# Last attention values moved between branch b's products, branch c run one product further ahead, and the norm's gain applied by ScalarE while it rounds

## The reference

```python
def second_block(x, mem, positions, ...):
    x = x + 0.5 * swiglu(rmsnorm(x, ffn1_norm[l]), ffn1_w_gu[l], ffn1_w_down[l])
    h = rmsnorm(x, mix_norm[l])
    z = h @ w_in[l]
    ...
    y_a = spatial_gating(u, v, ...)            # branch a
    y_b = mla(...)                             # branch b, 8 heads
    y_c = memory_attention(...)                # branch c, 4 heads
    merged = (gates[:, :, 0] * (y_a @ w_branch_a[l])
              + gates[:, :, 1] * (y_b @ w_branch_b[l])
              + gates[:, :, 2] * (y_c @ w_branch_c[l]))
    x = x + merged @ w_out[l]
    x = x + 0.5 * swiglu(rmsnorm(x, ffn2_norm[l]), ffn2_w_gu[l], ffn2_w_down[l])

def rmsnorm(x, g):
    y = x * rsqrt(mean(x * x, axis=-1) + EPS)
    return y * g
```

## Time and profile before

| what | value |
|---|---|
| time, median of 3 runs (lowest to highest) | 1173.15 us (1172.92 to 1176.21) |
| the profiled execution: time, span of the profile | 1176.21 us, 1174.5 us |
| PE busy | 1106.4 us, 94% of the span |
| DVE, ACT, POOL busy | 694.7, 591.0, 440.2 us (59%, 50%, 37%) |
| mean granted clock of TensorE | 0.971 of full speed |
| DMA | 204.91 MB, mean 174 GB/s |

### The profile page before, as it was taken

One profiled execution on the slowest core, in us unless ns is written; L12 is line 12 of the kernel. 1 busy time (PEld: TensorE's weight loads), 2 busy tenths in 40 slices (PEclk: granted clock), 3 DMA queues, 4 the chain that ended last, 5 costly groups with the idle time before them and its releaser, 6 DMA issues.

```text
span 1174.5 us, 21772 instructions
## 1 busy us (share of the span) xinstructions
PE 1106.4 (94%) x8468; PEld 1065.5 (91%) x8468; DVE 694.7 (59%) x1122; ACT 591.0 (50%) x1041; POOL 440.2 (37%) x236
## 2 busy tenths in 40 slices
PE   4789999899989999999999999999999887999999
PEld 3669999778889999999999998999899887999998
DVE  6545878887668843337777423665766774444421
ACT  4436565564455554444444445697544345444432
POOL 5440112112544544434444453323323244444442
PEclk8889999899989999999999999999899998999999
DMA  9546977213435555555555554444233343555553
GB/s 366 211 144 222 355 264 271 92 56 125 162 128 183 189 183 179 182 178 180 181 185 185 186 179 137 168 137 169 99 120 132 120 153 126 188 179 180 183 186 117
DMA packets 57651, 204.91 MB, mean 174 GB/s; under 512 B 6959, under 2 KB 8367, under 8 KB 57432
## 3 DMA queue, kind: packets, MB, share of 16 engines
q1 hardware_dynamic: 51176, 180.53, 45.0%
q0 software_dynamic: 6384, 23.09, 5.5%
HBM read 202.53 MB, written 1.06 MB: 173 GB/s over the span
## 4 chain that ended last, share of the span: by engine, by line
PE 79%; DVE 9%; DMA 4%; ACT 3%; issue 2%; POOL 1%; SPq 1%; DVEq 0%; ACTq 0%; POOLq 0%
PE bank L613 79%; DMA ring<-in_stream 2%; DMA ada_ring<-in_ada 2%; DVE ring_rounded L1610 1%; DVE ada_acc L1687 1%; PE bank L867 1%; ACT rounded_rounded L1215 1%; POOL ring_rounded L1140 1%; ACT wide L1397 1%; DVE wide L1858 1%; DVE shared L2125 1%; DVE wide_rounded L1887 0%; DVE shared_rounded L1887 0%; SPq L567 0%; DVE stats L1853 0%
## 5 line engine op out<-in xcount | busy, mean ns | idle before, releaser
L1140 POOL TENSOR_TENSOR ring_rounded<-ring,rounded_rounded 128x1024 fp32r<-128x1024 f32 x154 | 386.5, 2510 | 595.5 <-ACT rounded_rounded L1215 595.5
L613 PE MATMUL bank<-u_rounded,rounded_rounded 128*128 128x256 f32 x1528 | 442.9, 290 | 6.1 <-ACT u_rounded L1272 3.8
L613 PE MATMUL bank<-u_rounded,ring_rounded 128*128 128x256 f32 x1528 | 436.3, 286 | 0.0
L613 PE MATMUL bank<-u_lo_rounded,rounded_rounded 128*128 128x256 f32 x1528 | 430.8, 285 | 0.0
L1215 ACT ACTIVATE rounded_rounded<-ring 128x1024 fp32r<-128x1024 f32 x326 | 340.9, 1053 | 166.8 <-PE bank L613 146.5
L1610 DVE TENSOR_TENSOR ring_rounded<-ring,rounded_rounded 128x1024 fp32r<-128x1024 f32 x172 | 255.5, 1487 | 213.2 <-ACT rounded_rounded L1215 212.8
L613 PEld LDWEIGHTS bank<-u_rounded,rounded_rounded 128*128 128x128 f32 x1528 | 297.8, 195 | 10.9 <-issue 9.7
L613 PEld LDWEIGHTS bank<-u_rounded,ring_rounded 128*128 128x128 f32 x1528 | 297.7, 195 | 0.1
L613 PEld LDWEIGHTS bank<-u_lo_rounded,rounded_rounded 128*128 128x128 f32 x1528 | 294.1, 194 | 1.4 <-DVE u_lo_rounded L1656 0.4
L613 PE MATMUL bank<-shared_rounded,rounded_rounded 128*128 128x256 f32 x992 | 256.6, 286 | 2.8 <-DVE wide L1900 2.6
L613 PE MATMUL bank<-wide_rounded,rounded_rounded 128*128 128x256 f32 x864 | 234.7, 287 | 18.3 <-DVE shared_rounded L1887 5.7
(11 more groups left out here) (273 smaller groups left out, 1149.5 us busy)
## 6 DMA issues: line engine op xcount, KB each, us to landing
ring<-in_stream SPq DMA_DIRECT2D x328, 512.0 KB, 3.3
ada_ring<-in_ada POOLq DMA_DIRECT2D x33, 512.0 KB, 5.6
wide<-in_mem_t SPq DMA_DIRECT2D x2, 512.0 KB, 5.9
shared<-in_ada POOLq DMA_DIRECT2D x2, 512.0 KB, 10.0
ada_ring<-in_ada SPq DMA_DIRECT2D x2, 512.0 KB, 13.7
x<-in_x_t SPq DMA_DIRECT2D x1, 1024.0 KB, 14.1
wide<-in_ada POOLq DMA_DIRECT2D x2, 512.0 KB, 21.4
wide<-in_ada SPq DMA_DIRECT2D x2, 512.0 KB, 21.5
```

The source lines that it names most:

```text
L613: return nc.tensor.matmul(out, lhs, rhs, start=start, stop=stop, skip_group_check=True)
L1140: pool.tensor_tensor(R(w), w, R(slot_round(q)), ALU.subtract).then_inc(slot_split_by_pool, 1)
```

## The change

Five edits:

1. PE: head i = 11's `values(10)`, `turn(11)` and `values(11)` no longer stand behind branch b's eight products but in front of `br_b3`, `br_b5` and `br_b7`; DVE's `split_output` of `memo2` and `memo3` moves in front of the gates of `br_b4` and `br_b7`.
2. PE and the weight stream: branch c's products stand in groups of 3, 2, 2, 1 (`C_BEFORE`) and not of 2, 2, 2, 2 before the steps of w_out.
3. The slot work of branch c's and `mix2_`'s tiles stands behind a tile's own work on DVE and ACT, not in front.
4. `add_and_split`: ACT rounds x times gain to u straight from x, with the gain as its per-partition scale, and only then squares; DVE's multiplication by the gain is gone, and its low part is one `scalar_tensor_tensor` (x times gain minus u).
5. The counters of `u_normed` are shifted for the row after ROW_2, which no longer counts there.

```diff
+C_BEFORE = ((0, 1, 2), (3, 4), (5, 6), (7,))
...
                     for m in range(KD):
+                        if m == 3:
+                            values(10)
+                        if m == 5:
+                            turn(11)
+                        if m == 7:
+                            values(11)
                         project(f"br_b{m}", 4, (attn_b, attn_b_lo2), ...)
                 if i < 11:
                     scores(i + 1)
-                if i:
-                    values(i - 1)
-                turn(i)
+                    if i:
+                        values(i - 1)
+                    turn(i)
...
-            values(11)
             for m in (0, 2, 4, 5):
                 claim(f"mix2_{m}")
             for k in range(KD // 2):
-                for m in (2 * k, 2 * k + 1):
+                for m in C_BEFORE[k]:
                     project(f"br_c{m}", 4, (attn_c, attn_c_lo2), ...)
...
             def round_merged(before, lo):
                 for m in range(KD):
-                    ahead(f"{'up_sb' if before == 0 else 'br_c'}{m}")
+                    if before == 0 or m == 0:
+                        ahead(f"{'up_sb' if before == 0 else 'br_c'}{m}")
                     act.wait_ge(merged_raw, before + m + 1)
                     a(R(merged[:, m, :]), lo[:, m, :], ACT.Copy).then_inc(merged_rounded, 1)
+                    if before and m < KD - 1:
+                        ahead(f"br_c{m + 1}")
...
-            def square_and_round(row, last, i):
-
-                taken(f"{last}{i}")
+            def round_and_square(row, last, i, gain, after):
+
+                if after is None:
+                    ahead(f"{last}{i}")
+                evacuated(act, f"{last}{i}")
+                a(R(u[:, i, :]), x[:, i, :], ACT.Copy, scale=col(gain, i)).then_inc(u_rounded, 1)
+                if after:
+                    ahead(after)
                 a(row_squares[:, i, :], x[:, i, :], ACT.Square).then_inc(row_squares_ready, 1)
-                act.wait_ge(u_normed, row * KD + i + 1)
-                a(R(u[:, i, :]), u_lo[:, i, :], ACT.Copy).then_inc(u_rounded, 1)
...
-                square_and_round(ROW_4, "mix2_", i)
+                round_and_square(ROW_4, "mix2_", i, "ffn2_norm_2", f"mix2_{min(i + 1, KD - 1)}")
...
-            def add_and_split(last, gate, gain, row):
+            def add_and_split(last, gate, gain, row, reach_later=False):
+
+                def low_part(i):
+                    dve.wait_ge(u_rounded, row * KD + i + 1)
+                    v.scalar_tensor_tensor(out=R(u_lo[:, i, :]), in0=x[:, i, :], scalar=gain[:, i:i + 1], in1=R(u[:, i, :]),
+                                           op0=ALU.mult, op1=ALU.subtract).then_inc(u_ready, 1)
...
                 for m in range(KD):
-                    add_residual(f"{last}{m}", m, gate(m), int(last == "mix2_" and m in (1, 3)))
-                    taken(f"{last}{m}")
-                    v.tensor_scalar(u_lo[:, m, :], x[:, m, :], gain[:, m:m + 1], None, ALU.mult).then_inc(u_normed, 1)
-                    for i in ([m - 1] if m else []) + ([m] if m == KD - 1 else []):
-                        dve.wait_ge(u_rounded, row * KD + i + 1)
-                        v.tensor_tensor(R(u_lo[:, i, :]), u_lo[:, i, :], R(u[:, i, :]), ALU.subtract).then_inc(u_ready, 1)
+                    if not reach_later:
+                        ahead(f"{last}{m}")
+                    add_residual(f"{last}{m}", m, gate(m), int(last == "mix2_" and m in (1, 3)), False)
+                    if m:
+                        low_part(m - 1)
+                    if reach_later:
+                        ahead(f"{last}{m}")
+                evacuated(dve, f"{last}{KD - 1}")
+                low_part(KD - 1)
...
                 if i == 11:
                     for m in range(KD):
+                        if m == 4:
+                            split_output(attn_c[:, 2, :], attn_c_lo2[:, 2, :], "memo2")
+                        if m == 7:
+                            split_output(attn_c[:, 3, :], attn_c_lo2[:, 3, :], "memo3")
...
             dve.wait_ge(branches_added, KD)
+            ahead("br_c0")
             for m in range(KD):
-                gate_branch(part[:, m % 2, :], 2 * KD + m, f"br_c{m}")
-                taken(f"br_c{m}")
+                gate_branch(part[:, m % 2, :], 2 * KD + m, f"br_c{m}", False)
+                evacuated(dve, f"br_c{m}")
                 v.tensor_tensor(merged_lo2[:, m, :], merged_lo2[:, m, :], part[:, m % 2, :], ALU.add).then_inc(merged_raw, 1)
                 if m:
                     rest_of_merged(KD + m - 1, m - 1, merged_lo2)
+                ahead(f"br_c{m}")
```

More of the change, by code:

```diff
@@ L1460, in _ @@
                     nc.scalar.preload_act_table_set("natural_log_exp_and_others")
-                square_and_round(ROW_2, "w2_", i)
+                round_and_square(ROW_2, "w2_", i, "ffn1_norm_2", None)
             row_inv("x2_ss")
@@ L1908, in _, with add_residual @@
             rest_of_merged(KD - 1, KD - 1, merged_lo1)
-            def add_residual(name, m, gate, half=0):
-                output(name)
+            def add_residual(name, m, gate, half=0, reach=True):
+                if reach:
+                    ahead(name)
+                full(dve, name)
                 free(v.scalar_tensor_tensor(out=x[:, m, :], in0=bank(name)[:, half * T:(half + 1) * T], scalar=gate, in1=x[:, m, :],
```

11 lines of the change are left out of this document (5 added, 6 removed).

## The result

| | before | changed |
|---|---|---|
| time, median of 4 runs (lowest to highest) | 1173.77 us (1172.92 to 1176.21) | 1165.39 us (1163.36 to 1166.14) |
| ratio, 95% interval | | 0.9925 (0.9905 to 0.9944) |
| the profiled execution: time, span | 1176.21, 1174.5 us | 1165.63, 1163.9 us |
| mean granted clock | 0.971 | 0.979 |

The change makes the kernel faster by 0.75%, 8.4 us (6.6 to 11.1 us by the interval). In another comparison of the same two kernels, with more rounds, it was 0.9918 (0.989 to 0.9946).

What follows compares the result with a forecast made beforehand. PE, busy 94% of the span, was held up by late DVE operations that lose time to POOL slots. Terms -7.1, +0.1, +0.1 and +0.45 gave -6.4 us: 1166.8 us from the median 1173.15, range 1160.8 to 1171.2.

Steps and rivals of the forecast that it cites:

- the forecast's: Whole kernel: the main case, 1165 to 1169 us, chance 0.53.
- Branch b to the steps: Branch b to `mix2_0`: earlier `values` and regrouped branch c shorten or remove PE's waits, -7.1 us.
- The half-chance of 0.45 us for `br_b7`'s addition: Branch b: if a POOL slot catches this addition, step 0 comes 0.9 us later; half was counted.
- a lone wait of 2.03 us: Before step 1 in the old kernel: such a wait was said to leave TensorE at 2.4 GHz.
- The norm behind `mix2_`: End of `mix2_`: last wait about 6.05 us for 5.95, +0.1, and +0.1 for `mix2_7`'s slot, which had no margin.
- the prediction's own signs of being wrong: Last wait shrinking to 3 us, a POOL wait before `mix2_7`, or step 0 still 2 us behind `br_c2`.
- The norm behind `w2_`: Last tile behind `w2_`: the square now stands behind the rounding and PE waits for it, +0.45 us.
- The pause only moves: Rival: in branch b the new order meets other POOL slots; only -2.2 us, 1171.0 us, chance 0.22.
- The end opens up as well: Rival: behind `mix2_`, x5 comes 2.5 to 3 us sooner, last wait halves; -10.8 us, 1162.4 us, chance 0.2.
- An end of the lock on one low part: Behind `mix2_`: x3's tile's low part escaping POOL's slot would bring x5 2.5 to 3 us sooner.

Runs made afterwards that it cites:

- e4: The changed kernel with the norm of before (square first, DVE's multiplication back, old slot places for `mix2_`): 1164.47 us, ratio to before 0.9931.
- e10: The kernel before with only `values`/`turn` moved among branch b's products and branch c grouped 3, 2, 2, 1: 1166.25 us, ratio to before 0.9934.
- b0: The kernel before, unchanged, timed against itself: 1173.45 us, ratio 0.9998.
- e5: The changed kernel with POOL's last addition of `mix2_`'s squares in front of its weight slot: 1164.24 us, ratio to before 0.9922.
- e7: The changed kernel with ACT's and DVE's weight slots up to `mix2_0`'s reach in front of the norm: 1164.99 us, ratio to before 0.9925.
- e11: The changed kernel with POOL's addition, DVE's tile 7 low part and ACT's last squares before slots, `mix2_0`'s slots before the norm, last squares before rounding: 1163.74 us, 0.9913.
- e0: The changed kernel again, no edit, in more rounds against the kernel before: 1164.84 us, ratio 0.9918.

## Why the prediction was right

The time was forecast as 1166.8 us and measured as 1165.39, inside the range, and the case that came is the forecast's. By the terms measured in the traces the sum is -7.6 + 0.5 + 0.4 = -6.7 us for -6.4: that it is so near is in part luck, since two errors of 0.5 and 0.3 us have opposite signs.

- **Branch b to the steps, -7.1 us.** Measured in the traces: -7.6 (e4, e10). Step 0 begins 19.26 us behind `br_b0` (19.4 forecast) after a wait of 1.04 (1.2), tile 7 waits 1.84 (1.8), there is none before step 1, and the clock is 1.00. The half-chance of 0.45 us for `br_b7`'s addition was not needed: the two last additions took 0.75 us together, and the missing term is the difference. Both edits pay, and add up.
- **The granted clock.** One reading was wrong, without consequence: that a lone wait of 2.03 us leaves TensorE at its upper level. In b0 the lower level stood right behind two such waits. What held in every trace with the new order is that waits of 1.02 and 1.84 us, with work between, left it at 1.00.
- **The norm behind `mix2_`, +0.2 us.** Right in sign and in who ends the last wait, the size was off: +0.5. The wait for `mix2_7`'s slot was put at 0.1 us; it costs 0.47 us, 0.24 of them as a wait named after POOL. That such a wait stands before `mix2_7` is one of the prediction's own signs of being wrong, and it came: the margin was rightly put at nothing, its price too low. x7 stands 0.4 us behind its product, not 1, which changed nothing, since POOL's chain ends the wait. The chain was as laid out: tile 3's low part caught (2.31 us), x5 1.4 us before `mix2_7`'s end (1.1 forecast), POOL's slot and then its shared addition, 6.0 us. ACT's rounding with the gain as pointer takes 0.509 us in the median where it took 0.42; the Trainium skill (ScalarE: Activation LUTs, What ACT_TABLE_LOAD costs) gives about 93 ns for a pointer operand, and by this row that is right.
- **The norm behind `w2_`, +0.45 us.** Measured +0.40.
- **The rivals.** "The pause only moves" did not come: `br_b6`'s addition met no slot. "The end opens up as well" did not come either, and e5, e7 and e11 show what opened the end: mostly POOL's addition in front of its slot and ACT's square in front of its own. An end of the lock on one low part, on which I had put it, was not needed (in e7 and e11 tile 2's takes 2.3 us in place of tile 3's); what it alone would bring no run shows.
- **The rest.** By the marks the change is worth 6.5 us (7.1 against b0) less 0.4 behind `w2_`: 6.1 to 6.7 us. The two comparisons say 8.4 and 9.6 us. Their intervals reach down to 6.6 and 6.3, and in the comparison with e0 all four kernels lie 1 to 3.5 us below their traces, the norm alone too (-1.3 for +1.3); in the later ones, on another chip, the two agree to 1.1 us (e4 -8.1 and -8.5, e10 -7.8 and -8.2). I hold some 6.5 us for the change's own; what the other 2 us are stays open, the chip among the possible reasons.

The Trainium skill (SBUF — State Buffer, SBUF: two separate sides) says that of a DVE operation with two SBUF inputs and a GpSimd operation the one that starts first holds the port pair for its whole length. The rows agree: DVE's additions that start under a slot end 0.3 us behind it (926.80 us for the slot's 926.52), those that read a bank stay at 0.42 us.

## What to carry to other kernels

When PE waits at several places for one chain of another engine, give the chain distance (a product more ahead of its consumer) before making its operations cheaper: the distance was worth 7.6 us here; the cheaper operations, with the order that came with them, cost half a microsecond at `mix2_` and 0.4 at `w2_`. At `w2_` the reason is in the order: the square that PE waits for stands behind the rounding. At `mix2_` the trace points the same way (the second square, and with it POOL's slot for `mix2_7`, stands behind ACT's slot), and no run isolates it. Look for what is queued in front of the last link on each engine (a slot of 2.4 us ahead of an addition of 0.7) and move that first. And after shortening one stretch, read the steady loop behind it again: a change ahead of it can set two engines' operations against each other for the rest of the loop.

## What the runs showed of the hardware that was not expected

- A DVE addition of 0.43 us took 2.11 us on average, 22 times in a row, when its start fell under POOL's slot of 2.5 us in each round of a loop; in the 13 other traces the same 22 additions took 0.43 us each.
- The same wait of 2.2 us in the same code was followed by a granted clock of 0.79 in one trace and 1.00 in others, 3 us of difference; and behind two waits of 6.01 and 5.92 us the next 4 us had 20 and 29 matmuls.
- Waits on other engines repeat to 0.02 us between executions while the whole time moves by several us: part of it is in the first 360 us, where a like matmul came from 4.0 us sooner (e0) to 2.4 us later (e5) than in the first trace of before, in code that is the same.
